# First attention: transposed value projections, a quarter at a time beside the tasks of the pair of heads ahead; the first FFN rows' residuals ahead of their row dots

## The reference

```python
def _forgetting_attention(h, w_in, b_f, w_o):        # layer 0, 16 heads of 64
    proj = h @ w_in                                  # q, k, v (1024 columns each) and 16 gates
    ...
    F = jnp.cumsum(log_sigmoid(gates + b_f), axis=1)
    s = q @ k.T / 8 + F[query] - F[key]              # per head, causal
    o = softmax(s) @ v
    return o @ w_o

def _conv_ffn(h, w_up, conv_w, conv_b, w_down):      # 1024 -> 2 x 2816 -> 1024
    u = h @ w_up
    conv = conv_b + sum(conv_w[j] * up[:, j:j + S] for j in range(3))
    gate, val = jnp.split(conv, 2, axis=-1)
    return (silu(gate) * val) @ w_down

x = x + g1 * attention(modulate(x)); x = x + g2 * _conv_ffn(modulate(x))
```

## Time and profile before

| | |
|---|---|
| profiled execution | 2388.44 us, span 2386.6 us |
| median of 3 runs | 2390.47 us |
| TensorE busy | 2293.8 us (96%), mean granted clock 0.988 |
| VectorE, ScalarE, GpSimd busy | 1541.0, 1146.3, 1209.4 us (65, 48, 51%) |
| chain that ended last | TensorE 80%, VectorE 12%, ScalarE 4% |
| first attention's tasks, pairs 1 to 6 | 164.75 to 567.59 us |
| VectorE in the FFNs, one operation | sum 0.70, first taps 1.28, residual 1.28 us |
| VectorE in pair 7, mean of one | low part of a task 0.56, row maximum 0.60, head pair's subtraction 1.22, normalization 0.69, 16 rows 1.22 us |
| first scores of pair 7's heads | 567.59 and 590.70 us |
| ScalarE in the FFNs, one operation | tap 1.21, copy of a product 0.60 us |

### The profile page before, as it was taken

One profiled execution on the slowest core, in us unless ns is written; L12 is line 12 of the kernel. 1 busy time (PEld: TensorE's weight loads), 2 busy tenths in 40 slices (PEclk: granted clock), 3 DMA queues, 4 the chain that ended last, 5 costly groups with the idle time before them and its releaser, 6 DMA issues.

```text
span 2386.6 us, 30699 instructions
## 1 busy us (share of the span) xinstructions
PE 2293.8 (96%) x10986; PEld 1909.2 (80%) x10986; DVE 1541.0 (65%) x2536; ACT 1146.3 (48%) x1993; POOL 1209.4 (51%) x1641
## 2 busy tenths in 40 slices
PE   5999999998998999999999999989999999999998
PEld 4778788787877888888888878987778888888886
DVE  6565756658789677777776577882775555555556
ACT  5365664746255333333333496771553333333333
POOL 1501312133557666667666562214376666666663
PEclk9999999999999999999999999989999999999999
DMA  6211211114621333344332323233111111111112
GB/s 264 63 49 36 69 38 50 45 45 176 222 96 58 111 124 124 124 128 124 121 123 93 106 71 78 54 109 130 36 45 53 54 53 53 54 53 54 54 54 80
DMA packets 69082, 207.20 MB, mean 87 GB/s; under 512 B 7729, under 2 KB 8369, under 8 KB 68802
## 3 DMA queue, kind: packets, MB, share of 16 engines
q1 hardware_dynamic: 35248, 121.13, 15.7%
q10 hardware_dynamic: 33682, 84.11, 11.0%
HBM read 186.92 MB, written 16.32 MB: 85 GB/s over the span
## 4 chain that ended last, share of the span: by engine, by line
PE 80%; DVE 12%; ACT 4%; issue 2%; DMA 1%; SPq 0%; ACTq 0%; DVEq 0%
PE bank L1063 50%; PE bank L753 18%; PE bank L892 1%; PE bank L918 1%; PE bank L953 1%; PE bank L928 1%; PE bank L1280 1%; PE bank L955 1%; PE bank L954 1%; PE bank L1220 1%; DVE ada_raw L1974 1%; DMA ada_raw<-in_ada_t 1%; ACT H L1405 1%; DVE bank L2064 1%; DVE PL L2090 1%
## 5 line engine op out<-in xcount | busy, mean ns | idle before, releaser
L1063 PE MATMUL bank<-H,w_spl 128*128 128x512 f32 x3552 | 824.2, 390 | 8.2 <-DVE X L2285 6.5
L1063 PEld LDWEIGHTS bank<-H,w_spl 128*128 128x128 f32 x3552 | 667.6, 188 | 151.8 <-DVE X L2285 9.3
L651 POOL TENSOR_TENSOR w_spl<-w_raw,w_spl 128x256 fp32r<-128x256 f32 x688 | 551.3, 829 | 408.1 <-ACT w_spl L1647 406.7
L1063 PE MATMUL bank<-TB,w_spl 128*128 128x512 f32 x2112 | 493.6, 390 | 1.6 <-DVE TB L2245 1.6
L753 PE MATMUL bank<-H,w_spl 128*128 128x512 f32 x1920 | 481.3, 397 | 5.2 <-DVE H L2424 2.5
L1063 PEld LDWEIGHTS bank<-TB,w_spl 128*128 128x128 f32 x2112 | 396.1, 188 | 85.8 <-issue 3.4
L753 PEld LDWEIGHTS bank<-H,w_spl 128*128 128x128 f32 x1920 | 354.7, 190 | 76.2 <-DVE H L2424 2.9
L1647 ACT ACTIVATE w_spl<-w_raw 128x512 fp32r<-128x512 f32 x328 | 196.4, 624 | 348.0 <-PE bank L1063 291.8
L590 POOL TENSOR_TENSOR pace<-one_s 128x1 f32<-128x1 f32 x49 | 13.7, 280 | 578.9 <-PE bank L918 352.4
L2276 DVE TENSOR_TENSOR bank<-bank,sU 128x512 f32<-128x512 f32 x80 | 55.9, 699 | 280.7 <-PE bank L1063 280.7
L2285 DVE SCALAR_TENSOR_TENSOR X<-bank,mods,X 128x1024 f32<-128x1024 f32 x160 | 204.7, 1279 | 34.6 <-PE bank L1063 33.9
(11 more groups left out here) (203 smaller groups left out, 3367.7 us busy)
## 6 DMA issues: line engine op xcount, KB each, us to landing
w_raw<-in_w_stream SPq DMA_DIRECT2D x184, 512.0 KB, 3.7
ada_raw_f<-in_ada_t ACTq DMA_DIRECT2D x136, 256.0 KB, 2.9
ada_raw<-in_ada_t SPq DMA_DIRECT2D x8, 1024.0 KB, 18.8
negF<-scratch_f ACTq DMA_DIRECT2D x16, 512.0 KB, 3.8
ada_raw_o<-in_ada_t ACTq DMA_DIRECT2D x4, 2048.0 KB, 8.1
ada_raw_o<-in_ada_t ACTq DMA_DIRECT2D x4, 1536.0 KB, 8.0
Hf<-scratch_o ACTq DMA_DIRECT2D x9, 512.0 KB, 4.5
X<-in_x_t SPq DMA_DIRECT2D x4, 1024.0 KB, 11.7
```

What stands on the lines that cost most here:

```text
L651: last = pool.tensor_tensor(block_at(layer, b, 1, q, q + 256), src[:, q:q + 256], block_at(layer, b, 0, q, q + 256).bitcast(F32), ALU.subt ...
L1063: last = pe.matmul(dst, block_at(layer, b, x, k * P, k * P + P), mov(y), start=(start and x + y == 0), stop=(stop and x == 1), skip_group_ ...
```

## The change

Values for the first two pairs are projected as before. From pair 2 on a pair has a value tile of its own, the weights are stationary and H moves: `v_step(r, i)` is 12 matmuls of 256 columns, half of the sum for a quarter (256 tokens) of 128 value columns, transposed. Eight such steps stand beside the tasks 14 to 21 of the pair ahead. ScalarE copies a quarter to SBUF (`copy_vt`, one task after it is done), TensorE transposes it back (`turn_v`, two tasks after, into the other half of the same bank), ScalarE and VectorE write V (`v_high`, `v_low`, three tasks after). The stretches between the groups are gone; Q and K are projected beside tasks 0 to 12 (FILL); the weight stream is put in that order. The loads of heads wait for the last value projection, and the lists of `o_low` and `out_first` are shifted. In the FFN's pair 2 two residuals come before the sums and taps, and in layer 0 its four row dots, with ScalarE's loads for the last two, come at the end; pair 3's first dot stands behind its first sum. Renamed helpers (`first_v_high`, `first_v_low`) do as before.

```diff
-MAX_V = [0, 0, 0, 3, 3, 3, 3, 0]
-MAX_K = (1, 4, 7)
 MAX_T = [[2, 1, 1, 1, 1, 1, 1, 2, 2, 0, 0, 0], [0, 0, 2, 1, 2, 1, 2, 1, 2, 1, 0, 0]]
-MAX_T.append(MAX_T[0])
-V_EARLY = 3
-V_TASK = 4 * NT - V_EARLY
+MAX_T += MAX_T
 PREFACE = 16
-FILL_1 = [2] * 16
-FILL_1_FIRST = [2] * 8
-FILL_2 = [0] * (2 * NT) + [1, 1, 1, 1, 1, 2] * 2 + [3, 2, 2, 2] * 2
+FILL = [3, 2, 2, 3, 2, 2, 2, 2, 2, 3, 3, 3, 3]
+FILL_FIRST = [2] * 8
+V_TASK = 14
...
-HEADS_SPLITS = {22: 0, 24: 1, 26: 2, 28: 3, 30: 4, 32: 5, 42: 6}
+HEADS_SPLITS = {26: 0, 27: 1, 29: 2, 31: 3, 33: 4, 35: 5, 42: 6}
...
-OUT_A_BESIDE = {25: (0,), 28: (1,), 31: (2,), 34: (3,), 37: (4,), 40: (5,), 44: (6,)}
+OUT_A_BESIDE = {28: (0,), 30: (1,), 32: (2,), 34: (3,), 37: (4,), 40: (5,), 44: (6,)}
...
-    return 6 * (pair // 2) + 4 * (pair % 2) + n % 4 // 2
+    return 3 * pair + (pair == 1) + n % 4 // 2
 def qk_steps(g, T):
-    if T < 2 * NT:
-        fill, done, first = (FILL_1, 0, 8 * g + 4) if g else (FILL_1_FIRST, PREFACE, 4)
-    elif g < NG - 1:
-        fill, done, first = FILL_2, 0, 8 * g + 8
-    else:
+    r, t = 2 * g + T // (2 * NT) + 1, T % (2 * NT)
+    fill, done = (FILL, 0) if r > 1 else (FILL_FIRST, PREFACE)
+    if 2 * r >= NH or t >= len(fill):
         return []
-    if T >= len(fill):
-        return []
-    a = done + sum(fill[:T])
-    return [(first + i // KT, i % KT) for i in range(a, a + fill[T])]
+    a = done + sum(fill[:t])
+    return [(4 * r + i // KT, i % KT) for i in range(a, a + fill[t])]
+def v_beside(g, T):
+    q, t = divmod(4 * NT * g + T, 2 * NT)
+    return [(q + 1, t - V_TASK)] if 0 <= t - V_TASK < 8 and 1 <= q < NH // 2 - 1 else []
+def v_quarter(g, T):
+    return [(r, i // 2) for r, i in v_beside(g, T) if i % 2]
...
                         if pr == 0:
-                            sp.wait_ge(qk_ps, 8 * NG)
+                            sp.wait_ge(v_ps, 8 + 4 * (NH // 2 - 2))
...
-                    if n >= 8 and n % 8 in (4, 5):
-                        pe.wait_ge(v_lo, 8 * (n // 8) + 7 + n % 2)
+                    if n >= 12 and n % 4 < 2:
+                        pe.wait_ge(v_lo, 8 + 4 * (n // 4 - 3) + 3 + n % 2)
...
-            def v_step(g, tt, between=True):
-                if tt == 0:
-                    pe.wait_ge(w_ready, 6 * g + 4)
-                if tt < 2:
-                    pe.wait_ge(qk_lo, 2 * (8 * g + 3 + tt))
-                else:
-                    pe.wait_ge(v_lo, 8 * g + tt - 1)
...
+            def v_step(r, i):
+                qd = i // 2
+                if i == 0:
+                    pe.wait_ge(w_ready, 3 * r + 3)
+                if i in (0, 2):
+                    pe.wait_ge(qk_lo, 2 * (4 * r + 3 + qd))
+                elif i % 2 == 0:
+                    pe.wait_ge(v_lo, 8 + 4 * (r - 2) + qd - 1)
+                last = product(bank(6 + qd % 2, 0, 256), w_tile(3 * r + 2), h_cols(256 * qd, 256),
+                               range(4 * (i % 2), 4 * (i % 2) + 4))
+                if i % 2:
+                    last.then_inc(v_ps, 1)
+            def turn_v(r, qd):
+                pe.wait_ge(vt_copy, 4 * (r - 2) + qd + 1)
+                for j in range(2):
+                    last = pe.transpose(bank(6 + qd % 2, 256 + j * P, 256 + j * P + P), vt[:, j * P:j * P + P], id_f[:])
+                last.then_inc(vt_ps, 1)
...
-                if T == 0:
-                    first.then_inc(w_used, 2 if g else 1)
+                if T % (2 * NT) == 0 and g + T != 2 * NT:
+                    first.then_inc(w_used, 1)
...
-                if T < NT:
-                    pe.wait_ge(v_lo, 8 * g + kb + 1 if g else 8)
+                if hl % 2 == 0:
+                    pe.wait_ge(v_lo, 8 + 4 * (h // 2 - 2) + kb // 2 + 1 if h >= 4 else 8)
...
             for g in range(NG):
-                for tt in range(V_EARLY, 8) if g else ():
-                    v_step(g, tt)
-                    if tt < V_EARLY + LAG:
-                        value(g - 1, 4 * NT - LAG + tt - V_EARLY)
                 for T in range(4 * NT):
                     hl, t = T // NT, T % NT
                     score(g, T)
                     if T >= LAG:
                         value(g, T - LAG)
-                    maxima = list(maxima_at(MAX_T[hl], t)) if hl < 3 else []
+                    elif g:
+                        value(g - 1, 4 * NT - LAG + T)
+                    for r, qd in v_quarter(g, T - 2):
+                        turn_v(r, qd)
+                    maxima = list(maxima_at(MAX_T[hl], t)) if 4 * g + hl + 1 < NH else []
                     steps = qk_steps(g, T)
                     while maxima or steps:
...
-                    if hl < 3 and t == 10:
+                    for r, tt in v_beside(g, T):
+                        v_step(r, tt)
+                    if 4 * g + hl + 1 < NH and t == 10:
                         turn_max(4 * g + hl + 1)
-                    if g < NG - 1 and T >= V_TASK:
-                        v_step(g + 1, T - V_TASK, False)
...
+            def copy_vt(r, qd):
+                act.wait_ge(v_ps, 8 + 4 * (r - 2) + qd + 1)
+                act.wait_ge(vt_ps, 4 * (r - 2) + qd)
+                nc.scalar.activation(vt[:], bank(6 + qd % 2, 0, 256), ACT.Copy).then_inc(vt_copy, 1)
+            def v_high(r, qd):
+                act.wait_ge(vt_ps, 4 * (r - 2) + qd + 1)
+                act.wait_ge(pv_ps, 2 * NT * (r - 1))
+                nc.scalar.activation(V[:, 2 * qd:2 * qd + 2, r % 2, 0:3:2, :],
+                                     bank(6 + qd % 2, 256, HALF).rearrange("p (t e d) -> p t e d", t=2, e=2),
                                      ACT.Copy).then_inc(v_hi, 1)
...
                 for T in range(4 * NT):
                     exp_task(g, T)
...
                         qk_high(n, 0)
                     for n in qk_done(g, T - 1) if T else []:
                         qk_high(n, 1)
-                    if g < NG - 1 and T > V_TASK:
-                        v_high(g + 1, T - V_TASK - 1)
+                    for r, qd in v_quarter(g, T - 1):
+                        copy_vt(r, qd)
+                    for r, qd in v_quarter(g, T - 3):
+                        v_high(r, qd)
...
                         high(0, 1)
                     next_high(p, 0)
                     next_high(p, 1)
-                    if p == NORMAL:
-                        load(0)
                     act.wait_ge(c_sum, n + 2)
                     tap(p, 0, pair(0))
-                    if p == NORMAL:
-                        load(1)
                     load(3)
                     u_copy_of(p, 6, sU, 3, n + 2)
                     load(4)
...
                     next_high(p, 2)
                     if p < PAIRS - 1:
                         next_high(p, 3)
+                    if p == NORMAL:
+                        load(0)
+                        load(1)
...
+            def v_low(r, qd):
+                dve.wait_ge(v_hi, 8 + 4 * (r - 2) + qd + 1)
+                V_.tensor_tensor(V[:, 2 * qd:2 * qd + 2, r % 2, 3:6:2, :],
+                                 bank(6 + qd % 2, 256, HALF).rearrange("p (t e d) -> p t e d", t=2, e=2),
+                                 V[:, 2 * qd:2 * qd + 2, r % 2, 0:3:2, :].bitcast(F32), ALU.subtract).then_inc(v_lo, 1)
...
-                    if g < NG - 1 and T > V_TASK:
-                        v_low(g + 1, T - V_TASK - 1)
+                    for r, qd in v_quarter(g, T - 3):
+                        v_low(r, qd)
...
-                    step(0)
+                    if p > NORMAL + 1:
+                        step(0)
                     if p > NORMAL:
                         sum_of(p, 1, 1, 0, ALU.add, sU)
+                    if p == NORMAL + 1:
+                        step(0)
                     if p % 2 == 0 and p > NORMAL:
                         low_part((p - 2) // 2, 0)
                         low_part((p - 2) // 2, 1)
-                    step(1)
                     if p > NORMAL:
+                        step(1)
                         step(2)
                     sum_of(p, 4, 3, 1, ALU.add, sU)
                     if p > NORMAL:
                         step(3)
                     taps(p, 0, pair(0))
                     if p == NORMAL:
-                        step(2)
-                        step(3)
+                        half_residual(p, 0)
                     step(4)
                     sum_of(p, 6, 4, 3, ALU.add, s5)
                     sum_of(p, 6, 4, 2, ALU.subtract, sU)
...
                         low_part(FT // 2 - 1, 0)
                     else:
                         step(5)
-                    half_residual(p, 0)
+                    half_residual(p, int(p == NORMAL))
                     taps(p, 1, pair(2))
-                    half_residual(p, 1)
+                    if p > NORMAL:
+                        half_residual(p, 1)
                     step(6)
                     gated(p)
                     half_residual(p, 2)
+                    if p == NORMAL:
+                        for i in range(4):
+                            step(i)
```

(77 more changed lines are left out.)

20 lines of the change are left out of this document (10 added, 10 removed).

## The result

The changed kernel takes 2398.06 us (median of 13 runs, 2393.65 to 2403.69) against 2390.4 for the kernel before (13 runs): a ratio of 1.0034, 95% interval 1.0026 to 1.0043. It is slower by 0.34%, 8 us; the forecast was slower, by 17. The profiled execution has a span of 2397.5 us against 2386.6: 10.9 us, where the medians lie 7.7 apart, so some 3 us of what the two profiles show are scatter between executions.

What follows compares the result with a forecast made beforehand. TensorE, working 96% of the first attention's stretch, was taken as the bound. Terms 12.5 + 6 + 3.5 - 3.3 - 1.4 = +17.3 us on the profiled 2388.44 gave 2406 us, range 2389 to 2420.

Steps and rivals of the forecast that it cites:

- the new wait: First attention, tasks T18 and T20: TensorE's v_step waits for VectorE's V subtraction, shown as 1.9 and 1.5 us idle.
- Work that moves: First attention, pairs 2 to 7: value matmuls keep their rate; 48 new transposes at 0.1 us each add 4.8 us.
- The waits: TensorE idle for V's low half at T18 and T20 of each pair window: 1.9 and 1.5 us.
- The openings: Start of each next pair in first attention: idle behind VectorE's 16 rows, taken as 0.25 us, between 0 and 1.25.
- Half clock: First attention: four of twelve new gaps drop TensorE to 1.2 GHz, 1.5 us each: +6 us, bounds 0 to 18.
- Tail: Last pair, q7: GpSimd's late split and VectorE's queue delay the second half's opening: +3.5 us, bounds 0 and 6.
- FFN 0: First FFN: pair 2's 5.11 us wait and half clock go, pair 3 gains two waits: -3.3 us, bounds -7.6 and 0.
- Rival D: First FFN: the residual wait only moves to pair 3's ScalarE copies, gain 0, total 2409; counted within the forecast's 64%.
- FFN 1: Second FFN, which has no row dots: both waits for the residual go, -1.4 us.
- A: First attention: the chain before v_step does not bind and the kernel is faster, -10.6 us, 2378; chance 9%.
- B: Waits come, but no clock drops, the tail stays hidden, first FFN gains its whole 7.6: +3.5 us, 2392; chance 15%.
- C: First attention: each of the twelve gaps brings a half-clock stretch, +12 us on the sum, 2418; chance 12%.

Runs made afterwards that it cites:

- the first two edits together: Changed kernel with V's rounding and low half one task earlier and first-FFN pair 3 loads behind ScalarE's copies: 2373.72 us, ratio 0.9941.
- the attention part alone: Changed kernel with the order changes in both FFNs taken back: 2398.96 us, ratio 1.0033 against the kernel before.
- the three edits together: Changed kernel with V split one task earlier, first-FFN loads behind copies, and six head pairs rounded before tile 26's split: 2372.23 us, ratio 0.9932.
- the first edit alone: Changed kernel with V's rounding (ScalarE) and low half (VectorE) one task earlier: 2378.27 us, ratio 0.9949 against the kernel before.

## Why the prediction was right, and where it was off

The sign and its main cause held: **the new wait** for VectorE's V subtraction in the turns T18 and T20, behind a chain that no average of busy time shows. 2398.06 lies in the range, 8 us under the figure. Term by term:

- **Work that moves**, forecast 65.57 us of work per window, measured 65.3. The transposes cost about what second attention's rows gave: 0.1 forecast, 0.08 for each when doubled. The Trainium skill ("TensorE: Matmul & The Clock Gate", "Part 4: PE-mode transpose") has some 275 ns for one in bf16 in a kernel's context; these, in fp32, are 0.27 us long in the changed kernel and cost 0.08, so the figure agrees as a length and not as a price.
- **The waits** were forecast as 1.9 and 1.5 and are 1.64 and 1.25. What was off is the arithmetic of the chain at T18: forecast 2.6 us from the start of the exponential to v_step, measured 2.40 (217.59 to 219.99), since ScalarE's copies followed one another in 0.53 and 0.27 us where 0.66 and 0.35 were taken. The forecast called VectorE's maxima hidden; they end together with the other leg, which changes nothing in the time and everything in the cure.
- **The openings**, forecast 0.25 each, cost 0 in the changed kernel: VectorE had 3 us of TensorE's waits to catch up in. With the waits away they come back at 0.45. Idle per window 3.0 against 3.65, work 0.27 less: +7.1 for the six windows instead of +12.5.
- **Half clock**, +6 forecast for four of twelve gaps: none. The granted clock is 1.00 in all six windows. This is the largest mis-sized term. The one gap of 1.96 before 143.63 was taken as like these, although a shorter gap lay close before it. The five other profiles with these waits (1.09 to 1.64 us, twelve in each) bear it out: of 72 in all, one brought the clock down, that at 426.57 in the run with doubled transposes. So a third was far too much. By the rule of the Trainium skill ("TensorE: Matmul & The Clock Gate", "A second HAM failure mode: psum-queue depth-cycling") all twelve would have brought it down; the trace doesn't agree, with twelve waits of 1.25 and 1.64 us and a granted clock of 1.00.
- **Tail**, +3.5 forecast, +4.5 measured. The mechanism is the forecast one: the first score of the second head, forecast 26.5 us behind the opening, stands 27.7 behind it (576.67 to 604.35, with the stretch at half clock in it), and the run that rounds the heads first shows that 2.4 us are the split ahead of the rounding. The rest is 1.5 us of half clock, which the forecast had not put in q7, and some 0.6 of VectorE's queue, which no run takes away by itself.
- **FFN 0**, -3.3 forecast, +1.3 measured in the profile. The term that was mis-sized is the price of a load. It was taken at 2.9 us from issue to landing, the median of all 136; these landed after 7.4:

```profile
ada_raw_f<-in_ada_t ACTq DMA_DIRECT2D x2, 256.0 KB, 7.4
```

  These are DMA issues of the changed kernel between 792 and 797. Together with them went the load of cbF (256 KB, landed after 6.9), issued just ahead, and one weight tile of 512 KB (6.6). The pair of loads issued alone at 787.55 landed after 2.8, so the median holds for loads without that company. The second wait became 5.09 instead of 2.4, both waits together 2.5 more than forecast, and 1.9 us of half clock followed (802.81 to 812.80 at a granted clock of 0.81). The size of the second wait changes from one execution to the next, 2.5 to 5.1 in the profiles with this code, while the landing stays between 6.3 and 7.4. Rival D, the wait that only moves to pair 3, was the true story of this part.
- **FFN 1**, -1.4 forecast, -2.1 measured. Both waits went as forecast. A wait costs a little more than the idle time shown for it: matmuls of 512 columns are shown as 0.39 us long and start 0.23 apart elsewhere, and this overlap of 0.16 is lost too. Two waits make 0.3 of the 0.7 by that; the rest isn't accounted for.

So 12.5 + 6 + 3.5 - 3.3 - 1.4 became 7.1 + 0 + 4.5 + 1.3 - 2.1, with a rest of -2.0 between the stages and a start 2.0 later, most of it scatter of the clock. That the sum came within 8 us is in part luck: the windows and their half clock were put 11.4 too high, the tail and FFN 0 5.6 too low. Rivals A, B and C are out as wholes. B's half, waits without a drop of clock, came true; its other half, a tail hidden and an FFN that gains all, did not.

## What to carry to other kernels

When a producer's result goes through other engines and back (product, copy, transpose, round, subtract), count in whose turn each hand-over stands and what is queued ahead of it, and put each step in the first turn in which its input is there. Here one task too late cost 18 us and turned a change worth 12 into a loss of 8. Where two legs of a chain end together, move both: one alone gives nothing. Price a load by what is issued together with it, not by the median of its kind, and when an operation is moved off a wait, look for the due time that the wait stood for.

## What the runs showed of the hardware

The same gap does not always lower the clock. A wait of 2.65 to 2.84 us before the first output projection step of q7 left its six matmuls at their usual length in the changed kernel and in one other run, and stretched them in five (2.26 to 2.90 us). The row of the changed kernel:

```profile
585.88 1.62 PE L760 MATMUL bank<-H,w_spl 128*128 128x512 f32 x6 [2.78 <-DVE H L2135]
```

That of the first two edits together, and the stretch behind it (PEclk is the number before the last two):

```profile
569.87 2.26 PE L760 MATMUL bank<-H,w_spl 128*128 128x512 f32 x6 [2.66 <-DVE H L2143]
```

```profile
569.80:573.00 3.20, 3.13 (x10) 2.57 (x11) 3.20 (x6) 0.00 (x0) 3.20 (x7) 0.63 0.99 406
```

In the changed kernel the drop came instead behind the next gap, 1.76 us before 594.43:

```profile
594.43:600.00 5.57, 5.57 (x21) 4.72 (x22) 5.45 (x15) 1.84 (x3) 2.69 (x4) 0.69 0.40 163
```

Both are stretches partly at 1.2 GHz and partly at 2.4. Gaps of 1.64 and 1.25 us some 8 us apart, in windows that are otherwise full, did it once in 72. The gap of 1.25 us before q1's opening did it in four of the twelve profiled executions, none of them that of the kernel before, from which the forecast read that such a gap keeps the clock. This is the score behind it with the attention part alone, 0.73 us long instead of 0.50:

```profile
164.05 0.73 PE L926 MATMUL bank<-QS,KS 128*128 128x512 f32 x1 [1.26 <-DVE QM L2100]
```

What tells the cases apart was not tried. For whoever compares two profiles it means that a few us, here 1.5 to 1.9 at a time, can stand in one of them by chance.

Small operations of VectorE grow beside GpSimd's work. The negation of the maxima (8 columns), in the three edits together, where GpSimd splits tile 26 from 570.57 to 576.39, and in the first edit alone, where GpSimd is idle then:

```profile
575.06 0.67 DVE L2101 TENSOR_SCALAR nmx<-mx 128x8 fp32r<-128x8 f32 x1
```

```profile
578.93 0.17 DVE L2091 TENSOR_SCALAR nmx<-mx 128x8 fp32r<-128x8 f32 x1
```

The Trainium skill ("Trainium Architecture — The Big Picture", "What this means for kernel authors") has VectorE and GpSimd contend for one shared pair of memory ports, as a lock. The rows fit that, as 0.50 of the 0.67 us is time that the same operation does not need alone; whether it is a lock they don't show.

Four times the length, 0.4 to 0.5 us on each of three such operations in a row: that covers the 0.61 us wait for the negation that appeared when the split was moved. The edit that took 2.4 us of q7 away brought this one.
